# Function-table loads of ScalarE put in other places of a two-network kernel on one Trainium2 core

## The reference

```python
def first_block(x, ...):                      # DEPTH = 2 layers
    for layer in range(DEPTH):
        mix = rg_lru_block(x, ...) if layer == 0 else stick_breaking_attention(...) @ attn_w_out
        x = layer_norm(DN_ALPHA * x + mix, ln_g[layer, 0], ln_b[layer, 0])
        f = conv_ffn(x, ...)                  # (gelu(h[..., :D_FF]) * h[..., D_FF:]) @ w_down, h a conv of x @ w_up
        x = layer_norm(DN_ALPHA * x + f, ln_g[layer, 1], ln_b[layer, 1])
    return x
```

```python
def rmsnorm(x, g):
    return x * lax.rsqrt(jnp.mean(x * x, axis=-1, keepdims=True) + RMS_EPS) * g

# layer 0 mixer: fourier_conv_mixer: in-projection, u = pu * sigmoid(pg), a 31-tap convolution,
#                rmsnorm and silu of it, a Fourier transform, out-projection
# layer 1 mixer: attn_mla_mixer: in-projection, rms norms of q, k, cq, ckv, rotary tables,
#                16 blocks of softmax(q k^T) v, out-projection
# each layer:    hier_moe: router softmax, top 2 of 32 experts, (silu(x Wg) * (x Wu)) Wd, combine
```

## Time and profile before

| | |
|---|---|
| median of three executions | 2369.89 us (2368.22 to 2370.47) |
| profiled execution, its own time | 2370.43 us |
| its span, first to last instruction | 2368.6 us |
| PE busy | 2189.4 us, 92% of the span |
| DVE busy | 850.2 us, 36% |
| ACT busy | 368.5 us, 16%, x695 |
| mean granted TensorE clock | 0.978 of full |

### The profile page before, as it was taken

One profiled execution on the slowest core, in us unless ns is written; L12 is line 12 of the kernel. 1 busy time (PEld: TensorE's weight loads), 2 busy tenths in 40 slices (PEclk: granted clock), 3 DMA queues, 4 the chain that ended last, 5 costly groups with the idle time before them and its releaser, 6 DMA issues.

```text
span 2368.6 us, 28099 instructions
## 1 busy us (share of the span) xinstructions
PE 2189.4 (92%) x10752; PEld 1346.7 (57%) x10774; DVE 850.2 (36%) x1774; ACT 368.5 (16%) x695; POOL 23.0 (1%) x26
## 2 busy tenths in 40 slices
PE   7999999979999999999999999998989888888887
PEld 6888887658888844555444444435546433333333
DVE  3466664043666659441211111103273311111112
ACT  2311112042111130220000000002222100000001
POOL 0000000000000000000000000010000000000000
PEclk9999999989999999999999999999999999999999
DMA  7556557412566681307999999976121599999994
GB/s 274 213 178 248 213 213 254 170 38 72 214 242 243 224 314 45 139 36 290 427 427 427 428 427 426 426 310 228 71 107 72 209 427 426 427 428 427 426 426 187
DMA packets 138472, 638.14 MB, mean 269 GB/s; under 512 B 7120, under 2 KB 10224, under 8 KB 104496
## 3 DMA queue, kind: packets, MB, share of 16 engines
q1 hardware_dynamic: 120928, 595.48, 62.8%
q0 software_dynamic: 5600, 21.27, 2.5%
q10 hardware_dynamic: 11888, 20.62, 2.4%
HBM read 606.41 MB, written 30.93 MB: 269 GB/s over the span
## 4 chain that ended last, share of the span: by engine, by line
PE 61%; DMA 24%; DVE 6%; issue 4%; ACT 3%; POOL 0%; SPq 0%; DVEq 0%; ACTq 0%; POOLq 0%
DMA ring<-in_exp_w_up 19%; PE T L700 15%; PE T L521 14%; PE T L585 7%; PE T L593 5%; DMA ring<-in_mod_w 4%; PE T L688 4%; PE T L723 3%; PE T L887 2%; DVE S L1342 1%; PE T L806 1%; PE T L552 1%; PE T L918 1%; DMA S<-y_rows,dst 1%; PE T L611 1%
## 5 line engine op out<-in xcount | busy, mean ns | idle before, releaser
L700 PE MATMUL T<-ring,S 128*64 128x512 f32 x2112 | 501.9, 630 | 73.1 <-DMA ring<-in_exp_w_up 70.5
L700 PEld LDWEIGHTS T<-ring,S 128*64 128x64 f32 x2112 | 155.9, 145 | 372.7 <-issue 367.1
L585 PE MATMUL T<-X,ring 128*128 128x256 f32 x1536 | 337.6, 379 | 0.7 <-ACT X L1053 0.7
L585 PEld LDWEIGHTS T<-X,ring 128*128 128x128 f32 x1536 | 290.9, 190 | 40.7 <-issue 1.6
L723 PE MATMUL T<-ring,S 128*64 128x512 f32 x1056 | 238.0, 592 | 1.2 <-DVE S L1546 1.2
L1342 DVE SCALAR_TENSOR_TENSOR S<-ring,cs,S 128x512 f32<-128x512 f32 x336 | 229.5, 746 | 0.0
L1540 DVE TENSOR_TENSOR S<-S,T 128x256 f32<-128x256 f32 x66 | 27.8, 422 | 498.7 <-ACT S L1121 498.7
L593 PE MATMUL T<-S,ring 128*128 128x256 f32 x768 | 176.7, 383 | 16.0 <-DVE S L1372 16.0
L688 PE MATMUL T<-S 128*128 128x128 f32 x1600 | 185.9, 277 | 5.6 <-DVE S L1421 5.6
L688 PEld LDWEIGHTS T<-S 128*128 128x128 f32 x1600 | 182.9, 193 | 6.5 <-DVE S L1421 3.4
L593 PEld LDWEIGHTS T<-S,ring 128*128 128x128 f32 x768 | 143.4, 190 | 51.6 <-DVE S L1372 33.3
(11 more groups left out here) (267 smaller groups left out, 1547.9 us busy)
## 6 DMA issues: line engine op xcount, KB each, us to landing
ring<-in_exp_w_gate SPq DMA_DIRECT2D x66, 2048.0 KB, 16.7
ring<-in_exp_w_up SPq DMA_DIRECT2D x66, 2048.0 KB, 21.1
ring<-in_exp_w_down SPq DMA_DIRECT2D x66, 2048.0 KB, 23.4
ring<-in_ffn_w_up SPq DMA_DIRECT2D x24, 2048.0 KB, 12.7
ring<-in_mod_w SPq DMA_DIRECT2D x24, 2048.0 KB, 8.0
ring<-in_ffn_w_down SPq DMA_DIRECT2D x12, 2048.0 KB, 7.9
y_rows<-S ACTq DMA_DIRECT2D x132, 128.0 KB, 7.6
y_rows<-zb POOLq DMA_DIRECT2D x4, 3072.0 KB, 22.6
```

The costliest lines, as they stand in the source:

```text
L585: ins = pe.matmul(T[:, m % 2, h * S:(h + 1) * S], w[:, k, m * P:(m + 1) * P], x1[:, k, :], start=(k == 0), stop=(k == KT - 1))
L700: ins = pe.matmul(T[c * B:(c + 1) * B, s, :].rearrange("p (g n) -> p g n", g=2), xgT[:, k, s * B:(s + 1) * B], ring[:, 3 * s:3 * s + 2, k ...
```

## The change

Every table load is written at a chosen place instead of being left to the builder at most of its places:

- Sqrt's load stands at the start of `layer_norm` and of `norm`, ahead of the squares, each time, whatever set is loaded.
- Gelu's load stands ahead of the loop of `ffn`; in the loop there is none.
- The load of the attention's set stands ahead of the evacuations of k and q instead of behind them.
- `norm` gets an argument `table`: that set is loaded right behind the square root (Sigmoid's in norm(0), Silu's in norm(1), Exp's in norm(2) and norm(4)). The load of Exp in `route` is gone.
- Exp's load for the softmax stands behind the last square roots of the mixer's norms instead of ahead of the first exponent.

```diff
             def layer_norm(i):
+                nc.scalar.preload_act_table(ACT.Sqrt)
                 for j in range(4):
...
             def ffn(l):
+                nc.scalar.preload_act_table(ACT.Gelu_apprx_tanh)
                 with act.Fori(0, NJ // 2) as i:
...
-            def norm(r, src, k_tiles=KT, n=N2, sq=S1, off=0, wait=None, shift=None):
+            def norm(r, src, k_tiles=KT, n=N2, sq=S1, off=0, wait=None, shift=None, table=None):
+                nc.scalar.preload_act_table(ACT.Sqrt)
                 for j in range(k_tiles // 2):
...
                 A(std[:, 0, 0:n // 4], T[:, 7, 0:n // 4], ACT.Sqrt, scale=1.0 / (k_tiles * P), bias=RMS_EPS).then_inc(n_std, 1)
+                if table is not None:
+                    nc.scalar.preload_act_table(table)
                 if shift is not None:
...
                 evac(u, lgT[:, 0:tt * P], in_=bank(u, tt * P)[0:36, :])
-                nc.scalar.preload_act_table(ACT.Exp)
                 for j in range(2 * tt):
...
             layer_norm(1)
+            nc.scalar.preload_act_table_set("natural_log_exp_and_others")
             for j in range(4):
                 evac(u0["k"] + j, kT[:, 2 * j:2 * j + 2, :], in_=pair(u0["k"] + j))
             for j in range(4):
                 evac(u0["q"] + j, qT[:, 2 * j:2 * j + 2, :], in_=pair(u0["q"] + j))
-            nc.scalar.preload_act_table_set("natural_log_exp_and_others")
...
-            norm(0, X, shift=(0, 0, 0))
+            norm(0, X, shift=(0, 0, 0), table=ACT.Sigmoid)
...
-            norm(1, S3, 4, sq=S1, off=4, wait=lambda k: act.wait_ge(yc_ready, k + 1))
+            norm(1, S3, 4, sq=S1, off=4, wait=lambda k: act.wait_ge(yc_ready, k + 1), table=ACT.Silu)
...
-            norm(2, X, sq=S2, wait=lambda k: read(act, u0["out_ab"] + k), shift=(0, 1, 1))
+            norm(2, X, sq=S2, wait=lambda k: read(act, u0["out_ab"] + k), shift=(0, 1, 1), table=ACT.Exp)
...
                 evac(u + 2 + j, cdr[:, j, :], func=ACT.Sqrt, scale=1.0 / P, bias=RMS_EPS)
+            nc.scalar.preload_act_table(ACT.Exp)
             u = u0["uq"]
...
-            norm(4, X, n=S, wait=lambda k: read(act, u0["out_cd"] + k // 2), shift=(1, 1, 3))
+            norm(4, X, n=S, wait=lambda k: read(act, u0["out_cd"] + k // 2), shift=(1, 1, 3), table=ACT.Exp)
```

## The result

The changed kernel takes 2356.11 us (median of six, 2353.64 to 2358.04), the kernel before 2370.18 us (median of six). The ratio is 0.9939, with a 95% interval of 0.9929 to 0.9949: 14.1 us less, where the interval allows 12.1 to 16.8 us. I had forecast 2359.3 us, a gain of 10.6, and a range down to 2356.5. So the sign held and most of the mechanism, the gain was larger than forecast, and the time lies 0.4 us under the range. The profiled execution took 2356.08 us, its span is 2354.3 us, its mean granted clock 0.982.

What follows compares the result with a forecast made beforehand. PE held 61% of the chain, DMA 24%, ACT 3%, so a load counts only on the chain. Terms -7.5 - 2.0 + 1.3 - 1.1 - 1.3 = -10.6 us gave 2359.3 us, range 2356.5 to 2364.0.

Steps and rivals of the forecast that it cites:

- Feed-forward, -7.5 us: Feed-forward loops: each of six turns gains 1.25 us without the load ahead of the copies; gelu's load before the loop is covered.
- Layer norms 1 and 3, -1.44: First and third layer norm: root's load moved ahead of the squares gains PE's wait at the spread, 0.72 us each.
- The four terms of 0.29 us: Layer norms 2 and 4, norm(4), norm(5): each gains the 0.29 us that the spread waits behind its filler.
- norm(0), +1.28: norm(0): the added Sqrt load stands on the path ahead of the squares and costs 1.28 us.
- norm(2), -0.53: norm(2): moving the root's load gains the 0.53 us that the spread waits behind its filler.
- norm(3), 0: norm(3): the spread follows the filler with no wait, so moving the load gains 0.
- Softmax, -1.28: Start of the softmax: Exp's load behind the first row maximum is on PE's wait of 3.07 us; removing it gains 1.28.
- My case for the clock: Rival: PE's shifted idle times add one low-clock stretch before dense matmuls, up to 4.3 us, 2363.6 us; chance 0.07.
- one sign of being wrong that I had named: Trace after, whole kernel: the prediction is wrong if the granted clock is low in places where it was full.
- Free reload: Rival at norm(0): loading the resident set is free, so norm(0) costs nothing; -11.9 us, 2358.0 us; chance 0.08.
- transfer-bound loop: Rival in the feed-forward: the second `mod_w` piece lands no earlier, so the 7.5 is gone; -3.1 us, 2366.8; chance 0.05.
- the long low clock behind norm(0): Slower case: clock stays low for 31 us from the dense in-projection after norm(0), giving 2374.6 us; chance 0.03.

## Why the prediction was right and wrong

The steps that failed are sizes of terms. In the four norms with six fillers the prediction took PE's shown wait of 0.29 us for the whole gain, and the runs showed 0.56 us in three of them and 0.63 in the fourth. In the softmax it took the load's 1.28 us and put the clock at nothing, and the runs showed 1.98. What is left lies mostly in low stretches of the clock elsewhere, and the range counted these upward only.

**Feed-forward, -7.5 us: right in mechanism, a little small.** The pair of the prediction's own profile gives -7.8, the means over six profiles each -8.0. The half without a load gave the distance to the issue to 0.01 us (14.62 and 14.63); the second L593 came at 25.13, earlier than in that half (25.35). Of my two ends for a turn, 0.99 and 1.28, the upper one was the truth: the whole chain moves up by the whole load. I had taken 1.25.

**Layer norms 1 and 3, -1.44: right in size** (-1.52), partly by luck. The filler behind the sums was taken as what is left, but after the change the spread still starts 0.06 us behind the reciprocal. The gain is what the root moved, 0.76 us each, and the shown wait of 0.72 happens to lie near it. This is the case that the prediction kept for its upper end, "0.8 if filler did not count".

**The four terms of 0.29 us (layer norms 2 and 4, norm(4), norm(5)): mis-sized.** The first three measured 0.56, norm(5) 0.63 between the means of its six old and six new profiles, together about 1.1 us more than forecast. The step that failed is reading the wait of the earlier trace rows as the whole gain. A wait behind filler is counted from a modelled end. In these three norms filler does bound the gain, since two fillers fewer gave the other 0.2 us. The signs of it stood in the rows: the squares' sums ended and the root could have started 0.8 us earlier, and 0.56 lies between this and the wait.

**norm(0), +1.28: right to the hundredth**, and PE's wait 2.11 us, as forecast. The squares start at 845.21, right behind 843.92 + 1.28.

**norm(2), -0.53: right** (-0.54). **norm(3), 0: right only at low clock.** The spread of the earlier trace rows takes 1.86 us, which is the low level; at full clock it follows a wait of 0.53 us as in norm(2), and there the edit gains about 0.5 us (combine and norm(3) 14.50 to 14.71 us with the old root, 13.76 to 14.16 with the new one). I took a row at one clock for all executions.

**Softmax, -1.28: mis-sized** (-1.98). "Nothing else is in the way" was the failed step. The clock was, by 0.7 us. The 1.09 us of L1018 stood in the earlier trace rows, and I didn't compare it with the same matmuls later in the softmax, which take 0.63. The load's own part is as forecast: PE's wait went from 3.07 to 1.80 us. The Trainium skill (page "ScalarE: Activation LUTs", section "What ACT_TABLE_LOAD costs") adds 1380 ns of draining to every switch to a different set. The trace disagrees again: taking away this switch shortened PE's wait by 1.27 us, and taking the switch on the chain out of each turn of the feed-forward loops gave back 1.28 us.

**The range.** With the stages as measured in the pair the sum is -12.85 us, and 2370.4 - 12.85 - 0.5 = 2357.1, inside my range. The last 1.0 us to the measured 2356.1 lies outside these stages, where low stretches differ and norm(3)'s edit may add its 0.5, and the executions of one kernel spread over 5 us here, over 10 for the kernel before. So whether the median falls inside or 0.4 us outside is partly chance. My case for the clock says that one stretch fewer gains as much, but the chances and the range counted only the loss. The range should have been wider on both sides. The price of one stretch was too high as well: the low stretch in norm(0) cost 0.6 us in one execution and 0.3 in another, where it fell on short matmuls between waits. The ten us of the earlier trace rows themselves cost no 4.3 us either: the attention took 45.82 us with them and 44.71 to 44.92 in the profiles with 3.4 us at the low level in the changed kernel. And one sign of being wrong that I had named came true: the clock was low in norm(0), where it had been full.

**The rivals.** Free reload and transfer-bound loop are refuted by experiment, the long low clock behind norm(0) by every profile: from the in-projection behind it to norm(2)'s sums it took 163.45 to 163.48 us in all of them, with no low stretch.

## What to carry to other kernels

A table load costs its 1.28 us only where the activation behind it is the last thing waited for; look for loads that the builder put behind a wait and into a loop, where six of them made 8.0 us of this gain of 14, and put them into a gap of ACT instead. Size the gain by comparing with a copy of the same code that lacks the suspect, as the second half of the turn, rather than by the wait that is shown: behind filler the wait shown can be too short (0.29 us for 0.56), and a low clock next to it adds to the price (0.7 us in the softmax). Where the granted clock falls differs between executions, so edits of 1 us are told by stages of the trace and not by the time of the whole.

## What I had not expected of the hardware

- Loading the set that is already loaded takes 1.28 us (843.92 to 845.21 at norm(0)), as each of the 36 loads of the kernel before does, whatever set it follows.
- All six profiles with the load at the softmax had a low stretch there, and one of six without it. L1018 and the next L1009 took 1.09 and 1.92 us in it, 0.63 and 1.02 at full clock, and the stage 0.7 us more than by the wait itself. In three of the six the clock was low already ahead of the longer wait, so the wait is not shown to be the cause.
- A matmul can start up to 0.17 us before the shown end of the filler ahead of it (389.97 against 390.14).
- In the router and experts of layer 0 a granted clock of 0.97 instead of 0.99 made the stage only 1.3 us longer, although L700 was busy 10.9 us longer over the whole program: it waited 10.5 us less for its weights.
